# Where the gate table is filled, what type the row numbers have, and who copies the first turned tokens, in a one-layer encoder step with 32 experts

## The reference, cut to what matters

```
le_sel = einsum('nge,ng->ne', le, one_hot(g_sel))   # top-1 of 4 groups
top_p, top_i = top_k(softmax(le_sel), 2)            # top-2 of 8 experts in it
gates = sum(one_hot(expert_id) * (p_g_sel * top_p)) # 32 experts in all
for e in range(32):
    gu  = hf @ w_e_in[e]                            # 1024 x 512
    act = silu(gu[:, :256]) * gu[:, 256:]
    out = out + gates[:, e:e+1] * (act @ w_e_out[e])   # 256 x 1024
y = rmsnorm(x + out, g_final)
```

## Time and profile before

| | |
|---|---|
| median of 3 runs | 608.01 us (607.6 to 609.07) |
| the profiled execution | 608.7 us, of which its span is 607.0 us |
| granted TensorE clock, mean | 0.969 |
| PE busy | 550.4 us (91%) |
| DVE busy | 286.4 us (47%) |
| ACT busy | 162.3 us (27%) |
| POOL busy | 120.7 us (20%) |
| moved by DMA | 148.94 MB |

### The profile page before, as it was taken

The page is one execution under the profiler, slowest core; times in us unless marked ns, Lnnn a source line. Parts: engine busy times, 40 slices in busy tenths (PEclk is TensorE's granted clock), DMA queues, the critical chain, the costliest instruction groups (busy, mean ns, idle before and its releaser), DMA issues.

```text
span 607.0 us, 7780 instructions
## 1 busy us (share of the span) xinstructions
PE 550.4 (91%) x3073; PEld 328.0 (54%) x3074; DVE 286.4 (47%) x489; ACT 162.3 (27%) x259; POOL 120.7 (20%) x184
## 2 busy tenths in 40 slices
PE   6999999999999898899999799999999777878983
PEld 5549999999765544444555573444443333333330
DVE  1452899999775645654535861211112110011147
ACT  3222212321765675643211111101010000001112
POOL 3141000302352332500200220221112111121002
PEclk9999999999998998899999879999999999889997
DMA  8902754400600700039743769999999999999994
GB/s 290 217 0 65 250 185 162 140 0 2 214 3 0 278 1 0 1 64 413 275 171 143 286 239 424 427 427 420 420 422 425 425 423 422 420 424 421 410 348 159
DMA packets 44188, 148.94 MB, mean 245 GB/s; under 512 B 7060, under 2 KB 23468, under 8 KB 35703
## 3 DMA queue, kind: packets, MB, share of 16 engines
q1 hardware_dynamic: 39687, 139.63, 59.7%
q0 software_dynamic: 4464, 8.80, 3.9%
HBM read 136.29 MB, written 19.59 MB: 257 GB/s over the span
## 4 chain that ended last, share of the span: by engine, by line
PE 66%; DMA 16%; DVE 7%; ACT 4%; SPq 4%; issue 2%; POOL 0%; DVEq 0%; POOLq 0%; ACTq 0%
PE ps L950 17%; PE ps L1355 10%; PE ps L1175 8%; DMA big<-in_w_expert_out 7%; PE ps L1380 6%; DMA low<-in_w_expert_out 5%; PE ps L912 5%; PE ps L1060 2%; DMA big<-y_dram 2%; SPq L596 2%; PE ps L1057 2%; PE ps L1019 2%; PE ps L1336 2%; DMA y_dram<-cw,low 1%; PE ps L1081 1%
## 5 line engine op out<-in xcount | busy, mean ns | idle before, releaser
L1760 DVE SCALAR_TENSOR_TENSOR big<-low,cwt,big 128x590 f32<-128x590 f32 x120 | 95.2, 854 | 0.4
L2134 DVE TENSOR_TENSOR low<-low,ps 128x256 f32<-128x256 f32 x16 | 6.7, 421 | 174.0 <-ACT low L1636 174.0
L1355 PE MATMUL ps<-big,low 128*64 128x512 f32 x320 | 85.0, 593 | 3.0 <-issue 2.1
L950 PE MATMUL ps<-cw_r 128*128 128x288 f32 x256 | 73.0, 295 | 0.0
L950 PE MATMUL ps<-low_r,cw_r 128*128 128x288 f32 x256 | 72.9, 294 | 0.0
L950 PE MATMUL ps<-cw_r,big_r 128*128 128x288 f32 x256 | 72.7, 294 | 0.0
L1175 PE MATMUL ps<-cw,low 128*128 128x512 f32 x128 | 56.7, 594 | 0.2 <-DVE low L1879 0.2
L1380 PE MATMUL ps<-big,low 128*64 128x512 f32 x176 | 41.8, 616 | 14.5 <-DMA big<-in_w_expert_out 9.5
L1355 PEld LDWEIGHTS ps<-big,low 128*64 128x64 f32 x320 | 29.8, 137 | 45.3 <-issue 45.2
L950 PEld LDWEIGHTS ps<-cw_r 128*128 128x128 f32 x256 | 47.4, 188 | 0.4 <-issue 0.4
L950 PEld LDWEIGHTS ps<-cw_r,big_r 128*128 128x128 f32 x256 | 47.2, 188 | 0.0
(11 more groups left out here) (274 smaller groups left out, 832.2 us busy)
## 6 DMA issues: line engine op xcount, KB each, us to landing
big<-in_w_expert_in SPq DMA_DIRECT2D x16, 2048.0 KB, 20.7
big<-in_w_expert_out SPq DMA_DIRECT2D x22, 1024.0 KB, 25.1
low<-in_w_expert_in SPq DMA_DIRECT2D x8, 2048.0 KB, 26.4
big<-in_w_in SPq DMA_DIRECT2D x20, 512.0 KB, 4.7
low<-in_w_expert_out SPq DMA_DIRECT2D x10, 1024.0 KB, 31.6
cw<-in_w_expert_in SPq DMA_DIRECT2D x4, 2048.0 KB, 28.5
big<-in_w_expert_in SPq DMA_DIRECT2D x6, 1024.0 KB, 35.7
y_dram<-big SPq DMA_DIRECT2D x9, 512.0 KB, 5.2
```

Source lines behind the costliest of these rows:

```text
L950: return pe.matmul(ps[:, proj_bank(j) + half, 0:HALF], w[:, k, :], h[:, k, cols], start=first, stop=last, skip_group_check=True)
L1355: mm = pe.matmul(ps[TILE * half:TILE * half + TILE, gu_bank(g), :], xt[:, k, TILE * half:TILE * half + TILE], wi[(2 * g + half) % WI_SLOTS ...
L1760: ins = dve.scalar_tensor_tensor(conv[:, i, :], u[:, i, j:j + CW], cwt[:, i, j:j + 1], conv[:, i, :], ALU.mult, ALU.add)
```

## The change

**Row numbers.** DVE's addition at L2082 now writes its two columns as int32 (`rows_of`, the same place in `tab`), and the indirect DMAs take their offsets from there. All of POOL's casts and gate copies go, with the semaphores `idx_ready`, `oidx_ready` and `gat_ready`; ACT takes the gate from `tab` itself. The last pair's row numbers are needed as float too, so DVE writes them once more (`last_rows`).

**Gate table.** `gate_table()` moves on PE from behind `turn(0)` to behind `gate_up(0)`, and `gates_in()` on DVE from behind `copy_xt(0)` to behind `copy_act_t(0)`. Its inputs `gentry` move to another part of SBUF, since `gate_up(0)`'s silu writes where they lay.

**First turned tokens.** DVE copies one half of `xt` for pair 0, ACT the other, and `gate_up(0)` waits for ACT's half ahead of its fifth step. **WARM** goes from 12 to 8. SP's list is the same.

```diff
@@ -51,7 +51,7 @@
 MEAN_AT = 26
 LAG = 4
 WSLOTS = 6
-WARM = 12
+WARM = 8
 HSLOTS = 3
 MORE_TURNED, MORE_XT, MORE_GU, MORE_SIL, MORE_ACT, MORE_ACT_TURNED, MORE_ACT_T, MORE_ROWS, MORE_SCALED = range(1, 10)
 MORE = MORE_SCALED
@@ -185,9 +185,10 @@
             return 7 if g == PAIRS - 1 else GU_BANK[g % RING]
 
         tab = rest[:, 1536:1536 + 4 * PAIRS].rearrange("p (g f) -> p g f", f=4)
-        idx = [rest[:, 1600 + b:1601 + b].bitcast(I32) for b in range(ROW_BUFS)]
-        oidx = [rest[:, 1604 + b:1605 + b].bitcast(I32) for b in range(ROW_BUFS)]
-        gat = [rest[:, 1608 + b:1609 + b] for b in range(ROW_BUFS)]
+        rows_of = tab[:, :, 0:2].bitcast(I32)
+        last_rows = rest[:, 1600:1601]
+        more_in = rest[:, 1604:1605].bitcast(I32)
+        more_out = rest[:, 1605:1606].bitcast(I32)
         more_tab = rest[0:TILE, 1612:1616]
 
         fill = cw[:, 0:576]
@@ -223,7 +224,7 @@
 
         place = [late(128 * c, 128).rearrange("p (k t) -> p k t", k=2) for c in range(NC)]
         entry = [late(640 + 128 * c, 128).rearrange("p (k f e) -> p k f e", k=2, f=2) for c in range(NC)]
-        gentry = [rest[:, 1024 + 64 * c:1088 + 64 * c].rearrange("p (k e) -> p k e", k=2) for c in range(NC)]
+        gentry = [late(640 + 64 * c, 64).rearrange("p (k e) -> p k e", k=2) for c in range(NC)]
         gex = late(1280, NC * NG)
         ex = late(1312, NC * NE)
         tmp = late(1472, NC * 2 * NE)
...
@@ -790,49 +788,29 @@
                 b = g % ROW_BUFS
                 if g >= ROW_BUFS:
                     pool.wait_ge(xg_turned, g - ROW_BUFS + 1)
-                pool.tensor_copy(idx[b], tab[:, g, 0:1]).then_inc(idx_ready, 1)
-                pool.wait_ge(idx_ready, g + 1)
                 pool.indirect_dma_start(
                     out=xg[b], out_offset=None, in_=h2_dram,
-                    in_offset=bass.IndirectOffsetOnAxis(ap=idx[b].bitcast(U32), axis=0),
+                    in_offset=bass.IndirectOffsetOnAxis(ap=rows_of[:, g, 0:1].bitcast(U32), axis=0),
                     bounds_check=COLS - 1, oob_is_err=False).then_inc(gathered[b], 16)
-
-            def gates(g):
-
-                if g >= ROW_BUFS:
-                    pool.wait_ge(yg_ready, g - ROW_BUFS + 1)
-                if g == 0:
-                    pool.wait_ge(tab_ready, 2)
-                pool.tensor_copy(gat[g % ROW_BUFS], tab[:, g, 2:3]).then_inc(gat_ready, 1)
 
             def scatter(g):
                 b = g % ROW_BUFS
                 if g >= ROW_BUFS:
                     pool.wait_ge(scattered[b], g // ROW_BUFS * 16)
-                pool.tensor_copy(oidx[b], tab[:, g, 1:2]).then_inc(oidx_ready, 1)
-                pool.wait_ge(oidx_ready, g + 1)
                 pool.wait_ge(yg_ready, g + 1)
                 if g == 0:
                     pool.wait_ge(y_cleared, 16 * 9)
                 pool.indirect_dma_start(
-                    out=y_dram, out_offset=bass.IndirectOffsetOnAxis(ap=oidx[b].bitcast(U32), axis=0),
+                    out=y_dram, out_offset=bass.IndirectOffsetOnAxis(ap=rows_of[:, g, 1:2].bitcast(U32), axis=0),
                     in_=yg[b], in_offset=None, bounds_check=2 * COLS - 1,
                     oob_is_err=False).then_inc(scattered[b], 16)
 
-            for g in range(ROW_BUFS):
-                gather(g)
-            for g in range(ROW_BUFS):
-                gates(g)
-            for g in range(ROW_BUFS, LAG):
+            for g in range(LAG):
                 gather(g)
             for g in range(LAG, PAIRS):
-
                 gather(g)
-                gates(g - LAG + ROW_BUFS)
                 scatter(g - LAG)
             for g in range(PAIRS - LAG, PAIRS - 1):
-                if g + ROW_BUFS < PAIRS:
-                    gates(g + ROW_BUFS)
                 if g == PAIRS - 3:
                     pool.wait_ge(xg_turned, PAIRS - 1)
                     iota(tokens, [[1, COLS]])
...
@@ -1332,6 +1310,8 @@
                 pe.wait_ge(gathered[g % ROW_BUFS], g // ROW_BUFS * 16 + 16)
                 if g >= 1:
                     pe.wait_ge(xt_ready, g)
+                if g == 1:
+                    pe.wait_ge(h2t_ready, NC + 1)
                 for k in range(KD):
                     mm = pe.transpose(ps[:, k // 4, P * (k % 4):P * (k % 4) + P], xg[g % ROW_BUFS][:, P * k:P * k + P], ident[:, :])
                 mm.then_inc(xg_turned, 1)
@@ -1345,6 +1325,8 @@
                 if g >= RING:
                     pe.wait_ge(act_ready, g - RING + 1)
                 for k in range(KD):
+                    if g == 0 and k == KD // 2:
+                        pe.wait_ge(h2t_ready, NC + 1)
                     if g >= PAIRS - HALVED and k == KD // 2:
                         for e in (2 * g, 2 * g + 1):
                             pe.wait_ge(wi_rest_loaded[e], 16)
@@ -1384,9 +1366,10 @@
                 mm.then_inc(y_done, 1)
 
             turn(0)
-            gate_table()
             for g in range(PAIRS - 1):
                 gate_up(g)
+                if g == 0:
+                    gate_table()
                 turn(g + 1)
                 turn_act(g)
                 down(g)
@@ -1639,12 +1622,15 @@
             def gated_rows(g):
                 b = g % ROW_BUFS
                 act.wait_ge(y_done, g + 1)
-                act.wait_ge(gat_ready, g + 1)
+                if g == 0:
+                    act.wait_ge(tab_ready, 2)
                 if g >= ROW_BUFS:
                     act.wait_ge(scattered[b], g // ROW_BUFS * 16)
                 act.activation(yg[b].rearrange("p (m n) -> p m n", m=2), ps[:, 4:6, :],
-                               ACT.Copy, scale=gat[b]).then_inc(yg_ready, 1)
-
+                               ACT.Copy, scale=tab[:, g, 2:3]).then_inc(yg_ready, 1)
+
+            act.wait_ge(xg_turned, 1)
+            act.copy(xt[:, KD // 2:KD], ps[:, 1, :].rearrange("p (k t) -> p k t", t=P)).then_inc(h2t_ready, 1)
             for g in range(PAIRS - 1):
                 silu(g)
                 gated_rows(g)
@@ -2079,7 +2065,8 @@
             dve.tensor_tensor(c3(ex), lg[:, :, NG:NG + NE], m1.unsqueeze(2).broadcast_to([P, NC, NE]), ALU.subtract).then_inc(gsub_ready, 1)
             dve.wait_ge(tab_summed, 1)
             sums2 = ps[:, 6, 0:2 * PAIRS].rearrange("p (f g) -> p g f", f=2)
-            dve.tensor_scalar(tab[:, :, 0:2], sums2, BIGF, None, ALU.add).then_inc(tab_ready, 1)
+            dve.tensor_scalar(rows_of, sums2, BIGF, None, ALU.add).then_inc(tab_ready, 1)
+            link(dve.tensor_scalar(last_rows, sums2[:, PAIRS - 1, 0:1], BIGF, None, ALU.add))
             dve.wait_ge(gexp_ready, 2)
             link(dve.tensor_reduce(gsum, c3(gex), AX.X, ALU.add))
             link(dve.reciprocal(pg, gsum))
@@ -2126,6 +2113,9 @@
                 dve.wait_ge(xg_turned, g + 1)
                 if g >= 1:
                     dve.wait_ge(gu_done, g)
+                if g == 0:
+                    dve.tensor_copy(xt[:, 0:KD // 2], ps[:, 0, :].rearrange("p (k t) -> p k t", t=P)).then_inc(xt_ready, 1)
+                    return
                 dve.tensor_copy(xt, ps[:, 0:2, :].rearrange("p b (k t) -> p (b k) t", t=P)).then_inc(xt_ready, 1)
 
             def gate_times_up(g):
@@ -2140,11 +2130,12 @@
                 dve.tensor_copy(gact_t, ps[:, 6, 0:2 * P].rearrange("p (k t) -> p k t", k=2)).then_inc(act_t_ready, 1)
 
             copy_xt(0)
-            gates_in()
             further_tiles()
             for g in range(PAIRS - 1):
                 gate_times_up(g)
                 copy_act_t(g)
+                if g == 0:
+                    gates_in()
                 copy_xt(g + 1)
 
             def more(n, e, t):
@@ -2160,7 +2151,7 @@
 
             dve.wait_ge(zero_ready, EARLY_CONST + 4)
             dve.wait_ge(y_done, PAIRS - 2)
-            dve.tensor_tensor(pick15, tokens, tab[:, PAIRS - 1, 0:1].broadcast_to([P, COLS]), ALU.is_equal).then_inc(places_ready, 1)
+            dve.tensor_tensor(pick15, tokens, last_rows.broadcast_to([P, COLS]), ALU.is_equal).then_inc(places_ready, 1)
             gate_times_up(PAIRS - 1)
             copy_act_t(PAIRS - 1)
 
```

More of the change, by code:

```diff
@@ L349, in build @@
         pool_passed = sem("pool_passed")
-        idx_ready = sem("idx_ready")
-        gat_ready = sem("gat_ready")
-        oidx_ready = sem("oidx_ready")
         gathered = [sem(f"gathered{b}") for b in range(ROW_BUFS)]
@@ L844, in more @@
                 pool.sem_inc(pool_passed, 1)
-                pool.tensor_copy(idx[0][0:TILE], more_tab[:, 0:1]).then_inc(more_idx, 1)
-                pool.tensor_copy(oidx[0][0:TILE], more_tab[:, 1:2]).then_inc(more_idx, 1)
+                pool.tensor_copy(more_in[0:TILE], more_tab[:, 0:1]).then_inc(more_idx, 1)
+                pool.tensor_copy(more_out[0:TILE], more_tab[:, 1:2]).then_inc(more_idx, 1)
                 pool.wait_ge(more_idx, n * 2 + 2)
@@ L850, in more @@
                     out=xg[0][0:TILE], out_offset=None, in_=h2_dram,
-                    in_offset=bass.IndirectOffsetOnAxis(ap=idx[0][0:TILE].bitcast(U32), axis=0),
```

(3 more changed lines are left out.)

## The result

The changed kernel takes **614.12 us** (median of 6 runs, 611.32 to 617.55), the kernel before 608.16 us beside it (6 runs, 607.6 to 609.07). The ratio is 1.0117, with a 95% interval of 1.0095 to 1.0139. The profiled execution has a span of 612.2 us instead of 607.0. (The prediction started from 608.01, the median of the first three of the six runs of the kernel before.)

A forecast was written before the change was run, and what follows sets the result against it. The DMA stream of weights was taken as the limit, not PE. A 6.9 us hole from the late wo 4, less 0.3 us won at the start, gives +6.6 us on 608.0: 614.6 us, range 611.5 to 617.5.

The forecast's parts named there:

- The stream is the limit, byte for byte: DMA stream in the expert part: each idle microsecond before 577 us is a microsecond at the end.
- The first gather 0.33 us earlier: First gather, without its cast: 0.33 us won, moving SP's issue of wi 5 from 356.16 to 355.83.
- `gate_up(0)` 1.1 us earlier, at 358.4: PE's first gate-and-up, by fewer identity matmuls and the half copy: starts near 358.4 instead of 359.49 us.
- The cover for ACT's half: ACT's half of the first token copy: off the path, covered by eight matmuls, 1.8 us.
- The gate table uncovered: Between `gate_up(0)` and `turn(1)` on PE: full 1.48 us uncovered, PE 0.4 to 0.6 us later from the second pair.
- SP issues wo 4 at 369.06: SP's queue, waiting for tab_ready 2: wo 4 issued at 369.06 instead of 359.81 us, 9.25 us later.
- A hole of 6.9 us, 6.6 lost: DMA stream empty from 363.5 to 370.4 us: 6.9 us, less 0.3 won at the start, 6.6 us lost.
- The clock: TensorE's clock ahead of the first gate-and-up: rises as before, despite four fewer identity matmuls; forecast with this has 0.55.
- the low clock: First gate-and-up starts at half clock, delaying tab_ready and the stream: 616.0 to 617.4 us; chance 0.30.
- the first rival: Clock stays low into the first gate-and-up: 616.0 to 617.4 us; chance 0.30.
- The filled gap: Loads issued earlier still fill the stream's gap, so no slower: 606.8 to 607.7 us; chance 0.06.
- the end that hangs on PE: Stream has room, so only the second pair's 0.4 to 0.6 us shift counts: 608.5 us; chance 0.09 with other slack.

The follow-up runs named there:

- single increment: Changed kernel, but SP waits for the first increment of tab_ready ahead of wo 4, not the second; 607.85 us, ratio 1.0011.
- half dose: Changed kernel, but wo 4 waits for the first increment of tab_ready, wo 5 and all that follows for the second; 612.56 us, ratio 1.0094.
- the kernel with the low clock: Changed kernel with WARM = 0, no identity matmuls ahead of the first turn; 616.00 us, ratio 1.0140.
- wo 4 early: Changed kernel, but SP issues wo 4 once the logits are done, wo 5 behind tab_ready's first increment, after wi 5; 606.05 us, ratio 0.9980.
- gate table alone: Kernel before, with only gate table and its copy moved behind the first gate-and-up, its inputs elsewhere in SBUF; 613.69 us, ratio 1.0106.
- gate table back: Changed kernel with gate table and its copy returned to their old places; 608.49 us, ratio 1.0026.

## Why the prediction was right

The forecast was 614.6 us in a range of 611.5 to 617.5, the median is 614.12: 5.96 us above the kernel before beside it, where +6.6 was forecast. The mechanism is the one that was forecast; some terms were mis-sized by a few tenths, most of them to the high side. The steps, one by one:

*The stream is the limit, byte for byte.* Right, and shown twice: by the single increment (hole closed, loss gone, PE's list untouched) and by the half dose (same time of issue behind the hole, 1.05 MB more in it, 2.0 us given back where 2.5 were due). The megabyte did flow (253 instead of 209 GB/s over 24 us is 1.06 MB); why it gave back 2.0 and not 2.5 us stays open.

*The first gather 0.33 us earlier.* It starts 0.90 us behind the row numbers instead of 1.17, so 0.27. It then took 3.5 us to land instead of 3.4, and as the row numbers were 0.16 us later in this execution, wi 5 was issued at 356.17, not at 355.83.

*`gate_up(0)` 1.1 us earlier, at 358.4.* 358.52. Counted from the row numbers it is 6.81 us instead of 7.94, 1.13 earlier. DVE's half copy took 0.69 us, 0.66 was assumed. The turn took 1.52 us. The cover for ACT's half was misread in the prediction: eight of the 16 matmuls are half of 7.09 us, 3.5 and not 1.8. That changes nothing, since ACT's copy took 0.58 us.

*The gate table uncovered.* The row has 1.46 us, 1.48 was assumed. But from the start of the first gate-and-up to the copy of the first activations it is 9.62 us instead of 8.49, so it added only 1.13 us to PE's way; the rest overlaps its neighbours' rows. The forecast had PE 0.4 to 0.6 us late from the second pair on. The second gate-and-up starts at 372.28 instead of 372.12 us, which is 20.57 us behind the row numbers in both kernels: PE neither won nor lost.

*SP issues wo 4 at 369.06.* 368.73. The delay was 8.92 us (8.76 counted from the row numbers), not 9.25: the copy of the first activations came 0.22 us earlier than the sum had it, by the gate table's overlap, and the way from it to SP was 0.1 shorter.

*A hole of 6.9 us, 6.6 lost.* Here the sum is a little off. The windows are empty from 364.0 to 369.5, where the sum had 363.5 to 370.4: first bytes flow 0.8 us behind the issue and not 1.3, though full rate takes until 371. The missing bytes were right: 2.80 MB in the sum, 2.8 in the windows over 24 us. What wasn't right is that all of them come back at the end: 6.6 us of bytes cost 5.85. Why the end gives back some tenths of a microsecond stays open. The loss at the last scatter is 6.01 us by the clock of the trace, 5.85 by the expert stretch. The end of the span moved by 5.2, since what follows the scatter, the read of `y_dram` and the last norm, took 0.8 us less in this execution.

*The clock.* It rose at about 357 us, as before, with a third fewer identity matmuls. The prediction gave no row that says that eight are enough; it gave this 0.55 of its chances and the low clock 0.30, so this step is in part luck. The range didn't hang on it: the kernel with the low clock ends at 616.0. These are two half microseconds of the changed kernel, which answer to the earlier trace rows:

```profile
356.50:357.00 0.50, 0.50 (x4) 0.50 (x3) 0.00 (x0) 0.00 (x0) 0.00 (x0) 0.50 0.49 164
357.00:357.50 0.50, 0.50 (x6) 0.40 (x4) 0.00 (x0) 0.00 (x0) 0.00 (x0) 0.96 1.76 360
```

So the first rival did not happen in the profiled execution. But it is real: without the matmuls it costs 2.86 us. Whether some of the slower runs, up to 617.55 us, are executions in which it happened wasn't tried; their mean clock is lower (0.959 and 0.960 in the two slowest, 0.970 in the fastest), which fits this as well as low stretches ahead of the experts.

*The two other rivals.* The filled gap and the end that hangs on PE are both out: the queues were empty for 5.5 us, and PE starts the second gate-and-up 20.57 us behind the row numbers in both kernels, while the end is 5.85 us apart.

## What to carry to other kernels

Where one queue issues all loads in a written order, every wait in it is a wait for everything behind it. When work is moved behind something, look up who waits for its semaphore count, and ask whether that wait wants this work or only an earlier increment of the same count; here SP needed the first, and the second now came 17 us behind it.

When transfers are the limit, count bytes: what is outstanding, at what rate, against when the next load is released. An engine that starts earlier gains nothing by itself there (PE's first gate-and-up came 1.1 us earlier here, and the kernel is slower), and a low clock or a late engine costs only what exceeds the queue's reserve, as in the one case that was tried here.

## What the runs showed of the hardware that was not expected

**A gather behind bulk loads waits for them.** With two megabytes issued ahead of it, the first gather took 7.2 us from its start, 3.5 with nearly empty queues, and 2.5 MB moved meanwhile; one megabyte issued 6.6 us ahead of it left it at 3.6.

**Two indirect DMAs back to back** start 1.58 us apart on POOL (352.61 and 354.19 us) without a cast between them, 2.32 with it (352.72 and 355.04).

**Transposes did not raise TensorE's clock**, in the one execution with 16 of them in a row: the clock was still at half 4.9 us into the next matmuls.

**The scatter of the runs differs by kernel.** The kernels in which the stream has no reserve when wi 7 is issued (changed: 6.2 us from lowest to highest; half dose: 6.4; wo 4 early: 7.6) scatter more than the one with a reserve (single increment, 2.7 us). That a reserve absorbs the variation of the routing stage doesn't explain it by itself: the changed kernel without identity matmuls has no reserve either and scatters by 1.9 us, the gate table alone by 3.7, and the gate table back, which has no hole, by 5.2. The cause stays open.
